# Prompt attention with transposed scores, and a first pass for the row maxima

## The reference, cut to what matters

```
def _dense_attention(q, k, v, qpos, kpos, frame_causal, fq=None, fk=None):
    s = einsum('bqhd,bkhd->bhqk', q, k) * d ** -0.5
    if fk is not None:                      # fox: 6 heads, d = 64
        s = s + F_q[..., :, None] - F_k[..., None, :]
    allowed = kpos <= qpos                  # fox; mla (4 heads, d = 96): the same in blocks of 64
    p = softmax(where(allowed, s, -1e30))   # over the keys
    return einsum('bhqk,bkhd->bqhd', p, v)  # v has 64 columns
```

## Time and profile before

| | |
|---|---|
| median of 3 runs | 3323.08 us (3322.79 to 3323.21) |
| the profiled execution's own time | 3319.49 us |
| its span | 3317.7 us |
| PE, DVE, ACT, POOL busy, share of the span | 90%, 47%, 30%, 26% |
| mean granted PE clock | 0.935 |

### The profile page before, as it was taken

The page is one execution under the profiler, slowest core; times in us unless marked ns, Lnnn a source line. Parts: engine busy times, 40 slices in busy tenths (PEclk is TensorE's granted clock), DMA queues, the critical chain, the costliest instruction groups (busy, mean ns, idle before and its releaser), DMA issues. The chain is left out here.

```text
span 3317.7 us, 50480 instructions
## 1 busy us (share of the span) xinstructions
PE 2993.8 (90%) x19996; PEld 2799.5 (84%) x19996; DVE 1575.9 (47%) x2735; ACT 992.2 (30%) x2175; POOL 860.9 (26%) x488
## 2 busy tenths in 40 slices
PE   7998877677999999999999998867679999999998
PEld 6997755456999999999899975636479999999998
DVE  3336655734344444444441474657333444444443
ACT  4224535534311111111232253445433111111111
POOL 3112141113422232223331123311143232222230
PEclk9998968788999999999999997788889999999999
DMA  5110100002511111111131101000034111111111
GB/s 182 37 42 22 40 11 18 1 9 63 169 58 38 51 50 38 40 49 43 51 102 47 41 2 40 10 17 1 13 98 149 51 38 51 38 51 38 51 51 53
DMA packets 181248, 161.79 MB, mean 49 GB/s; under 512 B 17236, under 2 KB 168316, under 8 KB 180860
## 3 DMA queue, kind: packets, MB, share of 16 engines
q1 hardware_dynamic: 181116, 160.02, 15.6%
HBM read 129.97 MB, written 30.13 MB: 48 GB/s over the span
## 5 line engine op out<-in xcount | busy, mean ns | idle before, releaser
L1954 PE MATMUL bank_b<-x_hi,fwhi 128*128 128x352 f32 x2112 | 690.1, 327 | 5.3 <-POOL fwlo L1910 5.3
L1954 PE MATMUL bank_b<-x_hi,fwlo 128*128 128x352 f32 x2112 | 688.4, 326 | 0.0
L1954 PE MATMUL bank_b<-x_lo,fwhi 128*128 128x352 f32 x2112 | 686.7, 325 | 0.0
L1910 POOL TENSOR_TENSOR fwlo<-raw,fwhi 128x1024 fp32r<-128x1024 f32 x132 | 321.9, 2439 | 583.3 <-ACT fwhi L2035 569.2
L1954 PEld LDWEIGHTS bank_b<-x_hi,fwhi 128*128 128x128 f32 x2112 | 399.4, 189 | 6.5 <-POOL fwlo L1910 5.9
L1954 PEld LDWEIGHTS bank_b<-x_lo,fwhi 128*128 128x128 f32 x2112 | 401.7, 190 | 0.0
L1954 PEld LDWEIGHTS bank_b<-x_hi,fwlo 128*128 128x128 f32 x2112 | 398.4, 189 | 0.6
L2143 DVE TENSOR_TENSOR fx<-fx,bank_b 128x352 f32<-128x352 f32 x528 | 275.3, 521 | 233.5 <-PE bank_b L1984 233.5
L1984 PE MATMUL bank_b<-fuhi,fwhi 128*128 128x352 f32 x1056 | 344.1, 326 | 10.2 <-DVE fx L2143 5.7
L1984 PE MATMUL bank_b<-fulo,fwhi 128*128 128x352 f32 x1056 | 344.5, 326 | 0.0
L1984 PE MATMUL bank_b<-fuhi,fwlo 128*128 128x352 f32 x1056 | 344.0, 326 | 0.0
(11 more groups left out here) (410 smaller groups left out, 5965.8 us busy)
## 6 DMA issues: line engine op xcount, KB each, us to landing
raw<-in_w_ffn_up SPq DMA_DIRECT2D x88, 512.0 KB, 3.9
raw<-in_w_ffn_down SPq DMA_DIRECT2D x44, 512.0 KB, 3.6
wraw<-in_w_in SPq DMA_DIRECT2D x18, 984.0 KB, 5.4
xs<-x_between SPq DMA_DIRECT2D x16, 528.0 KB, 4.1
x_between<-xs SPq DMA_DIRECT2D x16, 528.0 KB, 2.6
fx<-x_between SPq DMA_DIRECT2D x2, 4224.0 KB, 13.3
raw<-in_w_out SPq DMA_DIRECT2D x16, 512.0 KB, 5.3
x_between<-fx SPq DMA_DIRECT2D x3, 1408.0 KB, 6.3
```

The source lines that it names most:

```text
L1910: pool.tensor_tensor(self.wlo[:, r], self.raw[:, o % 2], self.whi[:, r].bitcast(F32), ALU.subtract)\
L1954: last = pe.matmul(bank[:, first_bank + t, 0:TN], w[:, role, c, :], x[:, c, self.cols(t)], start=(c == 0 and m == 0), stop=(c == DC - 1 an ...
```

## The change

`attend_prompt` keeps swa. Fox and mla prompt attention go to a new function, `attend_keys`. It goes over halves `u`: pair `u // 2`, queries 0 to 511 for an even `u`, 512 to 1023 for an odd one. A half has steps `b`, one for each block of 128 keys: 4 in an even half, 8 in an odd one.

- First pass: one matmul (high x high) for 128 queries and up to 512 keys; DVE takes the row's negated maximum into `mc`, with the mask on the diagonal tile by `tensor_tensor_reduce`. It is done for half `u + 1` in the steps of half `u` (`hosted_units`), and so are the transposes of q and k (`hosted_tiles`).
- The maxima are transposed on PE to rows, and ACT and DVE write them (with rows of ones for fox) as further rows of q (`maxima`). K has rows of ones, F high and F low. So the bias is part of the score matmul.
- Scores are computed a second time, keys x queries, up to 512 queries wide; ACT exponentiates them to `pT`, and no probability is transposed or divided.
- The values' product takes `pT` as it is. Sums over the keys are kept by adding the exponentials block by block into `acc` (POOL for head 0, DVE for head 1); at the end of a half 8 matmuls with one column each make the denominators, 8 more spread the inverses, and DVE multiplies once (`denominators`, `inverses`, `divide`).
- The masks are made for the new orientation.

In each step `values(u, b - 1)` stand ahead of `first_pass(u + 1, ...)`.

```diff
-        act.activation(k.mfoxr[:, :], k.const[:, C_MFOX:C_MFOX + P], ACT.Copy)
-        act.activation(k.mmlar[:, :], k.const[:, C_MMLA:C_MMLA + P], ACT.Copy)
+        one = k.const[:, C_ONE:C_ONE + P]
+        act.activation(k.mfoxr[:, :], k.const[:, C_TRI:C_TRI + P], ACT.Copy, scale=-BIG, bias=BIG)
...
+def attend_keys(nc, k, kind, heads, kdim, x_tile, v_of, yT, yc, mask, maskr, frow=None):
...
+    NU, HALF = 2 * pairs, SEQ // 2
+    HT = HALF // P
...
+    nb = lambda u: HT * (u % 2 + 1)
+    first_col = lambda u, b: max(b - HT * (u % 2), 0) * P
+    def max_units(u):
+        if u % 2 == 0:
+            return [(e, j, 0, (j + 1) * P, True) for j in range(HT) for e in range(2)]
+        return [(e, j, a, w, a > 0) for j in range(HT) for a, w in ((0, HALF), (HALF, (j + 1) * P)) for e in range(2)]
+    def hosted_tiles(u, b):
+        p = u // 2
+        if u % 2 == 0:
+            return [(p, HT + 2 * b), (p, HT + 2 * b + 1)] if b < 2 else []
+        return [(p + 1, b)] if b < HT and p + 1 < pairs else []
+    def hosted_units(u, b):
+        if u + 1 == NU:
+            return []
+        units = max_units(u + 1)
+        if u % 2 == 0:
+            at = (0, 4, 10, 16, 16)
+        else:
+            at = (0, 0, 0, 0, 2, 4, 6, 8, 8)
+        return units[at[b]:at[b + 1]]
...
+    order = [("aux", 0, 0), ("aux", 0, 1)]
+    for u, b in steps:
+        if b == 1 and u:
+            order.append(("inv", u - 1))
+        order += [("s", u, b, 0), ("s", u, b, 1)]
+        if b == 0 and u:
+            order.append(("den", u - 1))
+        if b == nb(u) - 1 and u + 1 < NU:
+            order += [("aux", u + 1, 0), ("aux", u + 1, 1)]
...
+            what = order[n]
+            if what[0] == "aux":
+                pe.wait_ge(aux_hi, 2 * what[1] + what[2] + 1)
+                pe.wait_ge(aux_lo, 2 * what[1] + what[2] + 1)
+            elif what[0] == "s":
+                pe.wait_ge(expd, 2 * step_no[what[1:3]] + what[3] + 1)
+            elif what[0] == "den":
+                pe.wait_ge(inverted, what[1] + 1)
+            else:
+                pe.wait_ge(y_done, what[1] + 1)
...
+        def sum_up(eng, u, b, e, done):
+            n, c = step_no[(u, b)], first_col(u, b)
+            new = pT[:, n % NP, e, c:HALF]
+            eng.wait_ge(expd, 2 * n + e + 1)
+            if b == 1:
+                old = pT[:, (n - 1) % NP, e, :]
+                if u:
+                    eng.wait_ge(den_done, u)
+                if c:
+                    eng.tensor_copy(acc[:, e, 0:c], old[:, 0:c])
+                eng.tensor_tensor(acc[:, e, c:HALF], old[:, c:HALF], new, ALU.add).then_inc(done, 1)
+            else:
+                eng.wait_ge(done, sums_to(u, b) - 1)
+                eng.tensor_tensor(acc[:, e, c:HALF], acc[:, e, c:HALF], new, ALU.add).then_inc(done, 1)
...
+                for n, (rows, value) in enumerate(((kh[R0:K2].bitcast(F32), 1.0), (mtab[:, 0:HALF - P], 0.0),
+                                                   (kl[R0:K2].bitcast(F32), 0.0))):
+                    pool.memset(rows, value).then_inc(cleared, 1)
+                    pool.wait_ge(cleared, n + 1)
+                pool.tensor_copy(mtab[:, HALF - P:HALF], mask).then_inc(cleared, 1)
...
+                def first_pass(u, units):
+                    p, s = divmod(u, 2)
+                    for e, j, a, w, _ in units:
+                        n = unit[0]
+                        pe.wait_ge(x_hi, tile_no(p, HT * s + j) + 1)
+                        if n >= 2:
+                            pe.wait_ge(maxed, n - 1)
+                        if fox:
+                            pe.wait_ge(row_in[p % 2], 64 * (p // 2 + 1))
+                        pe.matmul(psS[:, n % 2, 0:w], qh[0:K1, s, e, j * P:(j + 1) * P], kh[0:K1, p % 2, e, a:a + w],
+                                  start=True, stop=True).then_inc(scored, 1)
...
+                def maxima(u):
+                    pe.wait_ge(maxed, unit_base[u + 1])
+                    for e in range(2):
+                        item = ("aux", u, e)
+                        bank_free(pe, item)
+                        for j in range(HT):
+                            last = pe.transpose(psT[0:NA, bank_of[item] % 2, j * P:(j + 1) * P], mc[:, u % 2, j, e, :],
...
+                def scores(u, b):
+                    p, s = divmod(u, 2)
+                    c, diag = first_col(u, b), b >= HT * s
+                    if b == 0:
+                        pe.wait_ge(aux_lo, 2 * u + 2)
+                        pe.wait_ge(x_lo, tile_no(p, HT * s + HT - 1) + 1)
+                    for e in range(2):
+                        item = ("s", u, b, e)
+                        bank_free(pe, item)
+                        out = psT[:, bank_of[item] % 2, :]
+                        keys = slice(b * P, (b + 1) * P)
+                        pe.matmul(out[:, c:HALF], kh[0:K2, p % 2, e, keys], qh[0:K2, s, e, c:HALF], start=True, stop=False)
+                        pe.matmul(out[:, c:HALF], kl[0:K2, p % 2, e, keys], qh[0:K2, s, e, c:HALF], start=False, stop=False)
+                        last = pe.matmul(out[:, c:HALF], kh[0:K2, p % 2, e, keys], ql[0:K2, s, e, c:HALF], start=False,
+                                         stop=not diag)
+                        if diag:
+                            last = pe.matmul(out[:, c:c + P], k.identr[:, :], maskr, start=False, stop=True)
+                        last.then_inc(s_done, 1)
+                def values(u, b):
+                    p, n, c = u // 2, step_no[(u, b)], first_col(u, b)
+                    pe.wait_ge(expd, 2 * n + 2)
+                    if b == 0 and u:
+                        pe.wait_ge(y_copied, u)
+                    for e in range(2):
+                        last = pe.matmul(psO[HD * e:HD * e + HD, c:HALF], v_of(2 * p + e, b), pT[:, n % NP, e, c:HALF],
+                                         start=(b == 0), stop=(b == nb(u) - 1), skip_group_check=True)
+                    last.then_inc(mixed, 1)
+                def denominators(u):
+                    item = ("den", u)
+                    bank_free(pe, item)
+                    for e, done in enumerate((sum0, sum1)):
+                        pe.wait_ge(done, sums_before(u + 1))
+                        for j in range(HT):
+                            at = e * HT + j
+                            last = pe.matmul(psT[:, bank_of[item] % 2, at:at + 1], acc[:, e, j * P:(j + 1) * P],
+                                             ones[:, 0:1], start=True, stop=True)
+                    last.then_inc(den_done, 1)
+                def inverses(u):
+                    item = ("inv", u)
+                    bank_free(pe, item)
+                    pe.wait_ge(inverted, u + 1)
+                    for j in range(HT):
+                        for e in range(2):
+                            last = pe.matmul(psT[HD * e:HD * e + HD, bank_of[item] % 2, j * P:(j + 1) * P],
+                                             rec[:, e, j:j + 1].broadcast_to([P, HD]), ident, start=True, stop=True)
+                    last.then_inc(inv_done, 1)
...
+                for u, b in steps:
+                    for p, i in hosted_tiles(u, b):
+                        turn(p, i)
+                    if b == 1 and u:
+                        inverses(u - 1)
+                    scores(u, b)
+                    if b == 0 and u:
+                        denominators(u - 1)
+                    if b:
+                        values(u, b - 1)
+                    first_pass(u + 1, hosted_units(u, b))
+                    if b == nb(u) - 1:
+                        if u + 1 < NU:
+                            maxima(u + 1)
+                        values(u, b)
+                denominators(NU - 1)
+                inverses(NU - 1)
...
+                    if n >= NP:
+                        act.wait_ge(mixed, n - NP + 1)
+                        act.wait_ge(sum0, sums_to(*steps[n - NP]))
+                        act.wait_ge(sum1, sums_to(*steps[n - NP]))
+                    for e in range(2):
+                        act.wait_ge(s_done, 2 * n + e + 1)
+                        act.activation(pT[:, n % NP, e, c:HALF], psT[:, bank_of[("s", u, b, e)] % 2, c:HALF], ACT.Exp)\
+                           .then_inc(expd, 1)
+                    if b == nb(u) - 1:
+                        if u + 1 < NU:
+                            maxima(u + 1)
+                        copy_out(u)
...
+                def first_pass(u, units):
+                    for e, j, a, w, diag in units:
+                        n = unit[0]
+                        dve.wait_ge(scored, n + 1)
+                        ps, m = psS[:, n % 2, 0:w], mc[:, u % 2, j, e, NA - 1:NA]
+                        if diag:
+                            if a:
+                                dve.wait_ge(maxed, n - 1)
+                            dve.tensor_tensor_reduce(ps, ps, mtab[:, HALF - w:HALF], -1.0, m if a else -BIG, ALU.add,
```

(37 more changed lines are left out.)

143 lines of the change are left out of this document (added).

## The result

The changed kernel takes 3598.4 us (median of 4 runs, 3593.4 to 3599.6), the kernel before 3323.1 in the same job: a ratio of 1.0825, with an interval of 1.0806 to 1.0844. Slower was forecast; 3437 us and a range of 3345 to 3500 were not enough. The profiled execution has a span of 3591.5 us, 273.8 more than before.

A forecast was written before the change was run, and what follows sets the result against it. PE's work was taken as the bound, growing from 35.5 to 40.1 us a fox pair, plus waits; fox +34.3 and mla +22.8, over two layers +114.2, with 3319.5 and 3.6 gave 3437 us, range 3345 to 3500.

The forecast's parts named there:

- The walk: Engine-by-engine timing of fox and mla halves with their waits, summing to 3437 us; chance 0.45.
- a rival: Even halves: PE's clock falls in the thin first pass, half their work at 1.2 GHz, +5 each, 3487 us; chance 0.15.
- the same columns as before: Fox second scores: priced by unchanged columns at 13.0 us a pair, masks 1.4 more.
- my 163.0: Whole fox stage: start, halves and end sum to 163.0 us against 128.7 before, +34.3.
- The denominators' 1.75 us: Each half's 8 one-column float32 matmuls: 16 weight loads at 0.11 each, 1.75 us.
- 11.6 + 2.65: Fox stage start: maxima at 11.6 us; from the first maxima transpose PE waits until 2.65 for step 0's scores.
- 35.5: PE's work for a fox pair before the change, 35.5 us; after it 40.1.
- 23.9 + 7.0 less 2.65: Fox stage's last half, hosting nothing, 23.9 us; end 7.0; less 2.65 before step 0's scores.
- Hidden waits: All waits inside the halves vanish: fox 134.8 us, mla 97.3, program 3350; chance 0.20.
- not slower: One-column matmul loads cost 0.03 not 0.11, -26 us, with waits hidden too 3323; chance 0.07.
- Two cycles an element: First pass: tensor_tensor_reduce takes twice as long, +38 us, 3475; chance 0.13.
- POOL and DVE did collide: Sums over keys: DVE stands during POOL's sum; hidden, adding nothing; if all exposed, +70 us; no chance given.

The follow-up runs named there:

- fillers in the first pass: Changed kernel plus one float32 matmul of 128 columns into a spare PSUM bank ahead of each first-pass matmul; 3561.3 us, ratio 1.0711.
- the kernel with 128: Changed kernel with second scores over 128 rows in fox and mla (before 67 and 97; zero rows), cleared with little waiting; 3530.8 us, 1.0623.
- the last kernel above: Changed kernel with 128 score rows, separate PSUM bank for denominators and inverses, first-pass units set singly, maxima of only the last 128 keys; 3425.2 us, 1.0309.
- the single spreading: Changed kernel with even halves' first-pass units set singly: ahead of the scores, between the two heads' scores, ahead of the values; 3569.5 us, 1.0730.
- the kernel with 96 rows and fillers: Changed kernel with fox second scores over 96 rows and an extra float32 matmul ahead of each first-pass matmul; 3521.0 us, 1.0592.
- short maxima and 128 rows: Changed kernel with second scores over 128 rows, DVE taking maxima of only the last 128 keys of each first-pass unit; 3457.2 us, 1.0393.
- own bank and spread first pass: Changed kernel with denominators and inverses in their own PSUM bank, even halves' first-pass units set singly; 96 fox rows 3511.1 us, 128 rows 3480.8.
- with ones: Changed kernel with separate denominator bank, denominators by two 512-column matmuls with 64 columns of ones as weights, no inverses' matmuls; 3531.9 us, 1.0624.
- with the first pass ahead: Changed kernel with the next half's first pass ahead of the values' sums in each step; 3612.1 us, 1.0857.

## Why the prediction was wrong

**The step that failed is the clock.** The walk took every PE duration from the earlier trace rows, at full clock, added 2 us in the first half of each stage for the half clock, and left the rest to a rival (0.15, +5 us in each of ten even halves, 3487). That rival's mechanism came true in the halves that it named (fillers in the first pass: 7.5 to 5.4 us, at 1.00 for 0.50). In the odd halves the clock fell by another that I had not thought of: "the same columns as before" was said of the second scores, without the rows (96 before, 67 after). Together they cost three times what the rival had for a fox stage (15 us).

**How large it is.** This is an estimate. Put the fox stage together from parts at or near full clock, out of several of the kernels above: the start as it is 16.85, the first half 21.3 (the fillers' kernel, 287.8 to 309.1), two odd halves of 27.1, two even ones of 25 to 27 (step 0 7.4 to 9.5, then 7.4, 5.4, 4.8), the last with the end 30.5. That is 173 to 177 us, so some 43 to 47 of the stage's 219.5 are the clock, and my 163.0 was 10 to 14 low for the rest. Of the clock's part, 28.6 is the scores' rows by the kernel with 128; the other 14 to 18 come with the first pass and the start of the halves, which the runs change only together with waits. If the second fox stage is like the first, the clock is 86 to 94 us of the 161 that the program is over the forecast. The rest of the 161 is the sizes below, mla's 36 among them, and 7 outside the stages.

**The walk nearly held where the clock did.** An odd half: 26.4 forecast, 27.1 measured. The first half: 18.7 without its 2 us for the half clock, 21.3 measured, with fillers. In an even half it had PE start step 1 at 10.05, step 2 at 16.5 and step 3 at 21.3, 6.5 and 4.8 us apart; measured at or near full clock 7.4 and 5.4. From step 3 to the next half's first scores, 4.9 forecast and 4.8 measured. The denominators' 1.75 us are right to the hundredth at full clock (timeline of the last kernel above, start and us):

```profile
381.81 1.89 PE L1163 MATMUL psDfox<-const,accfox 128*128 128x1 f32 x16
383.56 0.47 PE L1109 MATMUL psSfox<-khifox,qhifox 66*128 66x512 f32 x1
```

At half clock they are 3.26, and the four value matmuls of 512 columns take 1.91 to the next start for 1.01 (forecast 1.2).

**Sizes that were off.** The start to the first scores: 11.6 + 2.65 forecast, 16.85 measured; POOL's clearing took the 7.6 us that I gave it (280.32 less 272.79), and the maxima's transposes began at 13.6. A pair's PE work before, given as 35.5, adds up to 35.7. The stage's last half with its end: 28.3 forecast (23.9 + 7.0 less 2.65), 30.5 with the clock mostly up. A POOL sum of 512 columns: 1.04 forecast from a multiply by a broadcast, 1.27 measured; no PE wait came of it. Mla: 112.7 forecast, 129.9 and 131.6 measured, at a clock of 0.76 and 0.75. Its odd half was right (26.70 us at 1.00 for 26.9); over were the even half (28.89 at 0.70 for 22.9), the last with its end (33.17 at 0.79 for 28.3), the first (24.17 for 20.4) and the start. How this divides between clock and waits isn't known: the fillers raised the clock and gave 1.7 us, the single spreading, which takes waits away, 11.6.

**The rivals.** Hidden waits and "not slower" are refuted: without the clock's part the fox stage is over 170 us by the estimate above, and in the kernel nearest to hidden waits 156, for the 134.8 that I gave them. Two cycles an element is refuted by 757 ns. POOL and DVE did collide: in the kernel with 128 rows a DVE sum of 512 columns beside POOL's takes 1.26 us, and one of the same form in the changed kernel, where POOL's has all but ended, 0.69. It was hidden behind PE as I said.

**The rule.** The Trainium skill, "TensorE: Matmul & The Clock Gate", Part 1, says that sustained PE activity releases the throttle. The stalls and thin stretches here agree with it. The 22.45 us of unbroken PE busy time at 0.50 don't, if activity is read as busy time; there the measurement decides.

**What stays open.** Why an odd half's start with its denominators sometimes runs at full clock (5.09 us in the kernel with 128 rows) and sometimes not (8.50) wasn't tried. In the kernel with 96 rows and fillers the clock falls 0.5 us after the first denominators' matmul, and in the one with short maxima and 128 rows both odd halves start at 1.00 (5.09), so these loads alone don't explain it. How the other 14 to 18 us divide isn't known either, nor why 128 rows are better than 96 in the changed kernel.

## What to carry to other kernels

When a change makes an operand shorter, compare the rows of its matmuls with those of before, not only the columns: zero rows can be what keeps TensorE's clock up, and they cost no column. Price each new stretch at both levels of the clock, above all where PE waits between short matmuls or runs dense over fewer rows than before. Where the windows show a clock under 1.00 and a busy PE at once, try zero rows first, and up to 128: here they cost 2 us at the start of a stage and gave 28.6. Fillers show a cause, but they are work too: 72 of them in a fox stage gained 9.7 us.

## What the runs showed of the hardware

- Dense fp32r scores of 512 to 256 columns over 67 rows, with values of 64 columns each side by side, ran at 0.50 for as long as they lasted (22.45 us, PE busy throughout); with 96 or 97 rows the same steps ran at 1.00 (12.26, 12.29).
- The kernel with own bank and spread first pass took 3511.1 us with 96 and 97 rows and 3480.8 with 128. In the kernel before, 128 rows changed nothing, and 65 left PE at 0.50 for 14 us more at the start of the first fox stage.
- Eight float32 matmuls of one column (16 records, each with a 128x128 load) take 1.75 us at full clock and 3.26 at half, 0.109 and 0.204 a load.
- RECIPROCAL over 128x512 from PSUM takes 3.37 us on DVE, a multiply of that shape 0.69.
- A float32 sum of two 128x512 SBUF operands takes 0.69 us on DVE, 1.27 on POOL, and 1.26 on DVE beside POOL's.
- A changed kernel varies by 0.04% to 0.9% between executions (3531.2 to 3532.7 us with ones, 3597 to 3628 with the first pass ahead), the kernel before by under 0.3%.
